# A six-sublayer encoder trunk on one core: inputs and output laid out on the host instead of turned on the chip, and the first loads split

## The chip, the core and the metric

One core of a Trainium2 chip. The metric is the device time of one launch in microseconds (us), median of several runs. TensorE (PE) multiplies, ScalarE (ACT) and VectorE (DVE) work element by element, GpSimd (POOL) does a little copying, SyncE (SP) issues most of the DMAs. A name with a q behind it (SPq, ACTq) is the engine's own sequencer, on which its DMAs are issued.

## What is computed

256 tokens of width 1024, with 16 learned meta tokens ahead of them (272 columns), go through two layers. Each layer is a SwiGLU block, a mixer (stick-breaking attention in the first, sliding-window attention with sinks in the second) and another SwiGLU block, each between two RMS norms. Everything is float32.

```python
def swiglu(x, w_gate, w_up, w_down):
    return (jax.nn.silu(x @ w_gate) * (x @ w_up)) @ w_down

h = jnp.concatenate([meta, x], axis=1)
for i in range(DEPTH):                       # DEPTH = 2
    g = norm_g[i]
    f = swiglu(rms_norm(h, g[0]), ffn_w_gate[i, 0], ffn_w_up[i, 0], ffn_w_down[i, 0])
    h = h + 0.5 * rms_norm(f, g[1])
    m = mixer(rms_norm(h, g[2]))             # stick-breaking, then sliding window
    h = h + rms_norm(m, g[3])
    f = swiglu(rms_norm(h, g[4]), ffn_w_gate[i, 1], ffn_w_up[i, 1], ffn_w_down[i, 1])
    h = h + 0.5 * rms_norm(f, g[5])
return h[:, N_META:]
```

## The kernel before

The engines run programs written out by hand, each its own, and meet at semaphores. The residual stream `xT` lies with the 1024 features on the partitions, as 8 tiles of 128 features x 272 tokens (index `d` or `k`), so that every product contracts over partitions.

The weights come as 158 **panels** of 1 MB (128 x 2048 floats): a panel is 256 output columns of an input matrix with all 8 feature tiles, or 256 rows of an output matrix. `load` (L309) on SP brings panel g into one of two buffers `raw`, as soon as `conv_lo` has read the panel two before it. A panel of an input matrix is made of 1 KB runs in memory (256 floats of a row), a panel of an output matrix of 4 KB runs. Float32 products are made of two halves each: ACT casts a panel to `w_hi` (`conv_hi`, L403, two halves of 1024 columns), DVE subtracts it from the panel to get `w_lo` (`conv_lo`, L583), and PE adds three products, `w_lo*y_hi`, `w_hi*y_hi` and `w_hi*y_lo` (L887 to L889, and in the first panels of a sublayer L931, L933 and L940). The activations are split in the same way: ACT scales `xT` with the norm's gain into `y_hi` (L422), DVE makes `y_lo` (`y_low`, L594).

**The start.** SP issues the tokens (1 MB, one token per row, into `sq`) and then panel 0; panel 1 waits until the small tables have landed (L340). ACT issues four small DMAs: the first 256 columns of the constants (an identity and a matrix of ones), the meta tokens, the norm gains as 96 rows, and the sinks as one row. PE turns the tokens: for each feature tile one small and two full transposes into a PSUM bank (L902, L904), between them one transpose for the gains (L897) and one product with ones that spreads the sinks (L898). ACT casts panel 0, copies gains and sinks out of PSUM (L449, L450) and then makes `y_hi`; DVE makes `w_lo` of panel 0, then copies each turned tile to `xT` (L625) and follows with `y_low` of the tile before. PE takes panel 0 tile by tile (k from 0 to 7, with both output tiles), then panel 1, panel 2, the sum for the norm (L988), panel 3 and so on. The other 792 KB of the constants, which are first needed in the attention, are issued by ACT behind the last `y_hi` (L425).

**The end.** After the last product DVE updates `xT` tile by tile (L851, L859, with 256 tokens). PE turns each tile back (L1196) into four PSUM banks, one for each half of the tokens and half of the features; ACT copies three of them out (L578), DVE the last (L879), and SP stores each quarter (256 KB) when it is copied (L365).

```python
            for n, (a, half) in enumerate(OUT_PARTS):
                if n < 3:
                    sp_eng.wait_ge(out_a, n + 1)
                else:
                    sp_eng.wait_ge(out_d, 1)
                sp_eng.dma_start(out_v[a, :, 512 * half:512 * half + 512],
```

Of the kernel before, what the change touches and what calls it, by code (L numbers as in the profile page):

```python
# [25 lines left out]
P = 128  # L26
# [54 lines left out]
FEW = 2 * P  # L81
# [38 lines left out]
OUT_PARTS = [(0, 0), (1, 0), (0, 1), (1, 1)]  # L120
# [3 lines left out]
def build(nc, x_in, meta_in, norm_g, w_gate, w_up, w_down, sb_w_in, sb_w_out,  # L124
          swa_w_in, swa_sinks, swa_w_out, const_in, out):
    ctx = ExitStack()
    with ctx:
# [25 lines left out]
        g_rows = sb("g_rows", [DEPTH * 6 * KT, P])  # L153
        s_row = sb("s_row", [1, NH])
# [44 lines left out]
        def x_rows(t):  # L199

            return t[:].rearrange("p a b -> p (a b)")[:, 0:2 * D].rearrange("p (a n) -> p a n", a=2)

        def meta_rows(t):
            return t[0:META].rearrange("p a b -> p (a b)")[:, 0:D]

        few_landed = sem("few_landed")
        const_in_sem = sem("const_landed")
        x_landed = sem("x_landed")
        small_landed = sem("small_landed")
        raw_landed = [sem(f"raw_landed{i}") for i in range(RAW_SLOTS)]  # L210
# [3 lines left out]
        small_T = sem("small_T")  # L214
        small_ready = sem("small_ready")
        x_turned = sem("x_turned")
# [60 lines left out]
        out_turned = sem("out_turned")  # L277
        out_a = sem("out_a")
        out_d = sem("out_d")
# [25 lines left out]
        @block.sync  # L305
        def _(sp_eng):
            sp_eng.dma_start(x_rows(sq), x_in.rearrange("(a p) d -> p a d", p=P)).then_inc(x_landed, 16)

            def load(g, more, src):  # L309

                if g >= RAW_SLOTS:
                    sp_eng.wait_ge(lo_ready, 2 * (g - RAW_SLOTS + 1) + 2 * more)
                sp_eng.dma_start(raw[:, g % RAW_SLOTS, :].rearrange("p (k n) -> p k n", n=src.shape[-1]), src)\
                      .then_inc(raw_landed[g % RAW_SLOTS], 16)

            def columns(wt, i):

                return wt.rearrange("(k p) n -> p k n", p=P)[:, :, bass.ds(256 * i, 256)]

            def rows(wt, i):  # L320

                return wt.rearrange("(r c p) n -> p r c n", c=2, p=P)[:, bass.ds(i, 1)].rearrange(
                    "p r c n -> p (r c) n")

            def pairs(lo, n, body):

                with sp_eng.Fori(0, n // 2) as it:
                    for c in range(2):
                        body(lo + c, 2 * it, 2 * it + c)
                if n % 2:  # L330
                    body(lo + n - 1, 0, n - 1)

            for t in SUBS:
                if t.kind == "ffn":
                    j = t.part // 2
                    if t.u == 0:
# [5 lines left out]
                        with sp_eng.Fori(1, 11) as it:  # L342
                            load(2, 2 * it - 2, columns(w_gate[0, 0], it))
                            load(3, 2 * it - 2, columns(w_up[0, 0], it))
                    else:
                        with sp_eng.Fori(0, 11) as it:
                            load(t.g0, 2 * it, columns(w_gate[t.layer, j], it))
                            load(t.g0 + 1, 2 * it, columns(w_up[t.layer, j], it))
                    pairs(t.g_out, 11, lambda g, more, i: load(g, more, rows(w_down[t.layer, j], i)))
                else:  # L350
                    w_in, w_out = (sb_w_in[0], sb_w_out[0]) if t.kind == "sb" else (swa_w_in[0], swa_w_out[0])
                    if t.kind == "sb":
                        pairs(t.g0, t.n_in, lambda g, more, i: load(g, more, columns(w_in, i)))
                    else:
                        for i in range(t.n_in):
                            load(t.g0 + i, 0, columns(w_in, SWA_PANELS[i]))
                    pairs(t.g_out, t.n_out, lambda g, more, i: load(g, more, rows(w_out, i)))

            out_v = out.rearrange("(a p) d -> a p d", p=P)
            for n, (a, half) in enumerate(OUT_PARTS):  # L360
                if n < 3:
                    sp_eng.wait_ge(out_a, n + 1)
                else:
                    sp_eng.wait_ge(out_d, 1)
                sp_eng.dma_start(out_v[a, :, 512 * half:512 * half + 512],  # L365
                                 x_rows(sq)[:, a, 512 * half:512 * half + 512]).then_inc(out_stored, 16)
            sp_eng.wait_ge(out_stored, 64)
# [34 lines left out]
        def _(a):  # L402
            def conv_hi(g, it=0):  # L403
# [8 lines left out]
                for c in range(2):  # L412
                    part = slice(c * HALF, (c + 1) * HALF)
                    nc.scalar.copy(w_hi[:, g % SLOTS, part], raw[:, g % RAW_SLOTS, part]).then_inc(hi_ready, 1)  # L414
# [843 lines left out]
```

## Time and profile before

| | |
|---|---|
| median of 3 runs | 1123.28 us (1122.22 to 1127.62) |
| span of the profiled execution, first to last instruction | 1119.9 us |
| PE busy | 1080.2 us (96%) |
| DVE busy | 653.1 us (58%) |
| ACT busy | 503.3 us (45%) |
| PE's mean granted clock, as a share of full speed | 0.990 |
| read from memory, written | 167.78 MB, 1.05 MB |

The profiled execution is known by its span; the runs' times cover a little more than a span. The parts of the profile are: busy time of each engine, the chain of waits that ended last, groups of instructions by line, waits by who waited for whom, the DMA queues with the time from issue to landing, a timeline of instructions, and a table by stretches of time. Matmuls are pipelined, so the durations of neighbouring ones overlap; the distance of their starts tells the pace.

### The profile page before, as it was taken

To read this page: it belongs to the slowest core of one execution; us is meant where nothing else is said; L and a number is where in the kernel's file an instruction comes from. 1 tells how busy PE (TensorE), PEld (TensorE's weight loads), DVE (VectorE), ACT (ScalarE), POOL (GpSimd) and SP (SyncE) were. 2 spreads that over 40 slices of the span, in tenths; PEclk is the share of its full clock that TensorE was granted. 3 is DMA by queue.
4 is the path that set the end of the run, shared out by engine and by line. 5 is a ranking of instruction groups with operands and counts; after the bars stand their busy time and mean duration, and the time that the engine had idled before them with its cause. 6 is when DMAs were issued, how large, how long until landed. Compare 5 with 4: busy or idle time off the path is not lost.

```text
span 1119.9 us, 20564 instructions
## 1 busy us (share of the span) xinstructions
PE 1080.2 (96%) x8367; PEld 1045.7 (93%) x8367; DVE 653.1 (58%) x875; ACT 503.3 (45%) x710; POOL 10.9 (1%) x17
## 2 busy tenths in 40 slices
PE   7999999999999999999999999999997999999997
PEld 6999999899877899999998999999896789999996
DVE  5575553576565477555437765544687667755433
ACT  4554343444344455444334544433553746544422
POOL 0000000000000000000000000000011000000000
PEclk9999999999999999999999999999998999999998
DMA  7576555436300427654452665545340054765531
GB/s 232 177 229 188 166 173 188 150 114 225 113 1 1 151 77 225 186 187 156 183 186 78 189 211 165 186 169 170 113 152 37 4 186 125 236 202 187 188 113 38
DMA packets 125720, 169.62 MB, mean 151 GB/s; under 512 B 2674, under 2 KB 111442, under 8 KB 125666
## 3 DMA queue, kind: packets, MB, share of 16 engines
q1 hardware_dynamic: 125232, 167.78, 46.1%
q10 hardware_dynamic: 434, 1.06, 0.3%
q8 instruction: 41, 0.67, 0.3%
q14 instruction: 13, 0.11, 0.0%
HBM read 167.78 MB, written 1.05 MB: 151 GB/s over the span
## 4 chain that ended last, share of the span: by engine, by line
PE 93%; DVE 4%; ACT 1%; DMA 1%; issue 0%; SPq 0%; DVEq 0%; ACTq 0%
PE ps L887 25%; PE ps L889 25%; PE ps L888 25%; PE ps L1030 3%; PE ps L931 3%; PE ps L933 2%; PE ps L940 2%; PE ps L1048 1%; PE ps L1011 1%; PE ps L1113 1%; DVE w_lo L591 1%; PE ps L1182 1%; PE ps L1099 1%; DMA raw<-in_ffn_w_gate_dram 1%; PE ps L1084 1%; DVE scaled L851 0%
## 5 line engine op out<-in xcount | busy, mean ns | idle before, releaser
L414 ACT CAST w_hi<-raw 128x1024 fp32r<-128x1024 f32 x316 | 315.6, 1047 | 443.7 <-PE ps L889 337.6
L591 DVE TENSOR_TENSOR w_lo<-raw,w_hi 128x1024 fp32r<-128x1024 f32 x316 | 375.1, 1229 | 236.2 <-ACT w_hi L414 235.6
L887 PE MATMUL ps<-y_hi,w_lo 128*128 128x272 f32 (+1 forms) x1600 | 461.4, 288 | 2.9 <-DVE y_lo L737 1.0
L889 PE MATMUL ps<-y_lo,w_hi 128*128 128x272 f32 (+1 forms) x1600 | 459.8, 287 | 0.0
L888 PE MATMUL ps<-y_hi,w_hi 128*128 128x272 f32 (+1 forms) x1600 | 458.1, 286 | 0.0
L887 PEld LDWEIGHTS ps<-y_hi,w_lo 128*128 128x128 f32 x1600 | 301.3, 188 | 4.2 <-issue 3.5
L888 PEld LDWEIGHTS ps<-y_hi,w_hi 128*128 128x128 f32 x1600 | 301.4, 188 | 0.3
L889 PEld LDWEIGHTS ps<-y_lo,w_hi 128*128 128x128 f32 x1600 | 301.4, 188 | 0.0
L888 PE MATMUL ps<-h_hi,w_hi 128*128 (+2 forms) x704 | 201.6, 286 | 0.0
L887 PE MATMUL ps<-h_hi,w_lo 128*128 (+2 forms) x704 | 201.6, 286 | 0.0
L889 PE MATMUL ps<-h_lo,w_hi 128*128 (+2 forms) x704 | 200.9, 285 | 0.0
L887 PEld LDWEIGHTS ps<-h_hi,w_lo 128*128 128x128 f32 x704 | 132.7, 188 | 0.0
L889 PEld LDWEIGHTS ps<-h_lo,w_hi 128*128 128x128 f32 x704 | 132.5, 188 | 0.0
L888 PEld LDWEIGHTS ps<-h_hi,w_hi 128*128 128x128 f32 x704 | 132.4, 188 | 0.0
L931 PE MATMUL ps<-y_hi,w_lo 128*128 128x272 f32 (+1 forms) x224 | 60.2, 298 | 11.7 <-DVE y_hi L867 11.7
L650 DVE TENSOR_TENSOR hid<-act,ps 128x544 f32<-128x544 f32 (+1 forms) x44 | 31.2, 710 | 66.1 <-PE ps L889 66.1
L645 DVE TENSOR_TENSOR act<-ps,rms_inv 128x544 f32<-128x544 f32 (+1 forms) x44 | 31.5, 716 | 53.3 <-PE ps L889 49.1
L933 PE MATMUL ps<-y_hi,w_hi 128*128 128x272 f32 (+1 forms) x224 | 59.3, 294 | 0.0
L931 PEld LDWEIGHTS ps<-y_hi,w_lo 128*128 128x128 f32 x224 | 44.0, 196 | 14.0 <-DVE y_hi L867 13.8
L933 PEld LDWEIGHTS ps<-y_hi,w_hi 128*128 128x128 f32 x224 | 44.0, 196 | 0.0
L422 ACT ACTIVATE y_hi<-xT,gains 128x272 fp32r<-128x272 f32 (+1 forms) x43 | 22.3, 521 | 33.7 <-DVE xT L859 30.3
L940 PE MATMUL ps<-y_lo,w_hi 128*128 128x272 f32 (+1 forms) x224 | 35.6, 292 | 0.0
(106 smaller groups left out, 712.9 us busy)
## 6 DMA issues: line engine op xcount, KB each, us to landing
raw<-in_ffn_w_gate_dram SPq DMA_DIRECT2D x44, 1024.0 KB, 5.4
raw<-in_ffn_w_up_dram SPq DMA_DIRECT2D x44, 1024.0 KB, 5.4
raw<-in_ffn_w_down_dram SPq DMA_DIRECT2D x44, 1024.0 KB, 4.9
raw<-in_sb_w_in_dram SPq DMA_DIRECT2D x12, 1024.0 KB, 5.2
raw<-in_swa_w_in_dram SPq DMA_DIRECT2D x6, 1024.0 KB, 5.1
raw<-in_sb_w_out_dram SPq DMA_DIRECT2D x4, 1024.0 KB, 4.9
raw<-in_swa_w_out_dram SPq DMA_DIRECT2D x4, 1024.0 KB, 5.0
sq<-in_x_dram SPq DMA_DIRECT2D x1, 1024.0 KB, 5.8
```

The costliest lines, as they stand in the source:

```text
L414: nc.scalar.copy(w_hi[:, g % SLOTS, part], raw[:, g % RAW_SLOTS, part]).then_inc(hi_ready, 1)
L422: nc.scalar.activation(y_hi[:, d, t0:L], xT[:, d, t0:L], ACT.Copy, scale=gains[:, SUBS[b].pre + d:SUBS[b].pre + d + 1]).then_inc(yh_ready, 1)
L591: nc.vector.tensor_tensor(w_lo[:, g % SLOTS, part], raw[:, g % RAW_SLOTS, part], w_hi[:, g % SLOTS, part].bitcast(F32), ALU.subtract).then ...
L645: nc.vector.tensor_tensor(act[:, j % 2, :, t0:L], ps[:, b0:b0 + 2, t0:L], spread(rms_inv, 2, t0), ALU.mult).then_inc(gate_ready, 1)
L650: nc.vector.tensor_tensor(hid[:, j % 2, :, t0:L], act[:, j % 2, :, t0:L], ps[:, b0:b0 + 2, t0:L], ALU.mult).then_inc(h_ready, 1)
L887: nc.tensor.matmul(dst, w_lo[:, slot, pc], yh, start=first, stop=False)
L888: nc.tensor.matmul(dst, w_hi[:, slot, pc], yh, start=False, stop=False)
L889: return nc.tensor.matmul(dst, w_hi[:, slot, pc], yl, start=False, stop=last)
L931: nc.tensor.matmul(dst, w_lo[:, g % SLOTS, pc], y_hi[:, k, t0:L], start=(k == 0), stop=False)
L933: nc.tensor.matmul(dst, w_hi[:, g % SLOTS, pc], y_hi[:, k, t0:L], start=False, stop=False)
L940: nc.tensor.matmul(ps[:, BANK_IN[i][c], t0:L], w_hi[:, g % SLOTS, pc], y_lo[:, k, t0:L], start=False, stop=False)
L1030: mm = nc.tensor.matmul(ps[:, 2 + h % 2, at - back:at + width], cst("tri" if m == n else "ones"), sp[:, h % 2, src - back:src + width], st ...
```

## The change

All inputs are laid out on the host, ahead of the launch:

- The tokens come with the meta tokens ahead and already turned, as 128 x 8 x 272, in two DMAs straight into `xT` (tiles 0 to 3, tiles 4 to 7). The 28 transposes and products of the start, the PSUM copies L625, L449 and L450 and their semaphores are gone; `y_hi` and `y_low` of the first sublayer wait for the DMAs instead.
- Gains and sinks come as 128-partition tables by DMA (48 KB and 8 KB). The sinks are waited for only in the second attention.
- All 158 panels are one array in the order of use, each 128 rows of 8 KB. SP's program is five DMAs and then one loop with two loads a turn.
- Panel 0 is loaded in two halves, each with a semaphore, and the tokens' halves stand between and behind them. Panel 1 no longer waits for the small tables.
- All 920 KB of the constants are one DMA on ACT's queue, second in line at the start. PE waits for it ahead of the first norm sum.
- The output is stored as it lies, 8 stores of 128 KB, each when its tile of `xT` is updated; the host turns it back. The 16 transposes L1196 and the four copies L578 and L879 are gone.

```diff
 @block.sync
-            sp_eng.dma_start(x_rows(sq), x_in.rearrange("(a p) d -> p a d", p=P)).then_inc(x_landed, 16)
...
-                        load(0, 0, columns(w_gate[0, 0], 0))
-                        sp_eng.wait_ge(small_landed, 32)
-                        load(1, 0, columns(w_up[0, 0], 0))
...
+            sp_eng.dma_start(raw[:, 0, 0:HALF], panel(0)[:, 0:HALF]).then_inc(first_landed, 16)
+            sp_eng.dma_start(xT[:, 0:4, :], x_in[:, 0:4, :]).then_inc(x_landed[0], 16)
+            sp_eng.dma_start(raw[:, 0, HALF:PW], panel(0)[:, HALF:PW]).then_inc(raw_landed[0], 16)
+            sp_eng.dma_start(xT[:, 4:KT, :], x_in[:, 4:KT, :]).then_inc(x_landed[1], 16)
+            sp_eng.dma_start(raw[:, 1, :], panel(1)).then_inc(raw_landed[1], 16)
+            def load(g, it):
+                sp_eng.wait_ge(lo_ready, 2 * (g - RAW_SLOTS + 1) + 4 * it)
+                src = panels_in[bass.ds(2 * it + g, 1)].rearrange("g p n -> (g p) n")
+                sp_eng.dma_start(raw[:, g % RAW_SLOTS, :], src).then_inc(raw_landed[g % RAW_SLOTS], 16)
+            with sp_eng.Fori(0, PANELS // 2 - 1) as it:
+                for c in range(2):
+                    load(2 + c, it)
+            for d in range(KT):
+                sp_eng.wait_ge(x_ready, KT * 5 + d + 1)
+                sp_eng.dma_start(out[:, d, :], xT[:, d, META:L]).then_inc(out_stored, 16)
+            sp_eng.wait_ge(out_stored, 16 * KT)
 @block.scalar
-            a.dma_start(const[:, 0:FEW], const_in[:, 0:FEW]).then_inc(few_landed, 16)
-            a.dma_start(meta_rows(fT), meta_in).then_inc(x_landed, 16)
-            a.dma_start(g_rows[:], norm_g.rearrange("l n (k p) -> (l n k) p", p=P)).then_inc(small_landed, 16)
-            a.dma_start(s_row[:], swa_sinks).then_inc(small_landed, 16)
+            a.dma_start(gains[:], gains_in).then_inc(small_landed, 16)
+            a.dma_start(const[:], const_in).then_inc(const_in_sem, 16)
+            a.dma_start(sinks[:], sinks_in).then_inc(sinks_landed, 16)
             nc.scalar.preload_act_table_set("natural_log_exp_and_others")
+            a.wait_ge(first_landed, 16)
             conv_hi(0)
-            a.wait_ge(small_T, 1)
-            nc.scalar.copy(gains[:], ps[:, 7, 288:288 + 96]).then_inc(small_ready, 1)
-            nc.scalar.copy(sinks[:], ps[:, 7, 384:384 + NH]).then_inc(small_ready, 1)
-            a.wait_ge(small_ready, 2)
+            a.wait_ge(small_landed, 16)
             split_y(0)
 @block.vector
             conv_lo(0)
+            v.wait_ge(small_landed, 16)
             for d in range(KT):
-                v.wait_ge(x_turned, d + 1)
-                nc.vector.tensor_copy(xT[:, d, :], ps[:, d, 0:L]).then_inc(x_ready, 1)
...
+                v.wait_ge(x_landed[d // 4], 16)
+                y_low(0, d)
```

What now stands in two engines' programs. On DVE at the start, before (w_lo is the low half of the panels, y_lo that of the activations):

```order
L591 TENSOR_TENSOR w_lo<-raw,w_hi 128x1024 x2
L625 COPY xT<-ps 128x272 x2
L597 SCALAR_TENSOR_TENSOR y_lo<-xT,gains,y_hi 128x272
L625 COPY xT<-ps 128x272
L597 SCALAR_TENSOR_TENSOR y_lo<-xT,gains,y_hi 128x272
```

and in the changed kernel:

```order
L533 TENSOR_TENSOR w_lo<-raw,w_hi 128x1024 x2
L539 SCALAR_TENSOR_TENSOR y_lo<-xT,gains,y_hi 128x272 x8
L533 TENSOR_TENSOR w_lo<-raw,w_hi 128x1024 x4
L550 TENSOR_TENSOR fT<-fT 128x1088
```

The eight copies out of PSUM that stood between the `y_lo` steps are gone. On ACT at the start, the changed kernel has:

```order
L391 DMA gains<-in_gains_dram 128x96
L392 DMA const<-in_const_dram 128x1840
L393 DMA sinks<-in_sinks_dram 128x16
L394 ACT_TABLE_LOAD
L362 CAST w_hi<-raw 128x1024 x2
L373 ACTIVATE y_hi<-xT,gains 128x272 x8
L362 CAST w_hi<-raw 128x1024 x4
```

The large load of the constants, which stood behind the eight `y_hi`, has moved ahead of all of ACT's work; both casts of panel 0 still stand ahead of the first `y_hi`.

## Rows read from the trace of the kernel before

**Rows 1.** The page: busy time, and the two groups that split the panels.

```profile
PE 1080.2 (96%) x8367; PEld 1045.7 (93%) x8367; DVE 653.1 (58%) x875; ACT 503.3 (45%) x710; POOL 10.9 (1%) x17
...
L414 ACT CAST w_hi<-raw 128x1024 fp32r<-128x1024 f32 x316 | 315.6, 1047 | 443.7 <-PE ps L889 337.6
L591 DVE TENSOR_TENSOR w_lo<-raw,w_hi 128x1024 fp32r<-128x1024 f32 x316 | 375.1, 1229 | 236.2 <-ACT w_hi L414 235.6
```

**Rows 2.** Waits of PE: who waited for whom, us in total, times, longest.

```profile
PE ps L931 <- DVE y_hi L867: 11.7, 5, 2.4
PE ps L902 <- DMA fT<-in_meta_tokens_dram: 7.4, 1, 7.4
...
PE ps L887 <- DVE w_lo L591: 0.3, 1, 0.3
```

**Rows 3.** Timeline of the start: start us, duration us, engine, instructions, idle before.

```profile
0.75 0.44 SPq L307 DMA_DIRECT2D sq<-in_x_dram  x1
...
7.38 0.26 PE L902 MATMUL ps<-const,fT 16*128 16x16 f32 x1 [7.38 <-DMA fT<-in_meta_tokens_dram]
...
9.94 1.99 ACT L414 CAST w_hi<-raw 128x1024 fp32r<-128x1024 f32 x2 [5.78 <-DMA raw<-in_ffn_w_gate_dram]
...
11.01 2.36 DVE L591 TENSOR_TENSOR w_lo<-raw,w_hi 128x1024 fp32r<-128x1024 f32 x2 [11.01 <-ACT w_hi L414]
...
13.82 0.93 ACT L422 ACTIVATE y_hi<-xT,gains 128x272 fp32r<-128x272 f32 x2 [1.68 <-DVE xT L625]
...
14.40 0.59 PE L931 MATMUL ps<-y_hi,w_lo 128*128 128x272 f32 x1
...
15.47 0.66 PE L940 MATMUL ps<-y_lo,w_hi 128*128 128x272 f32 x2
...
18.64 0.43 PE L931 MATMUL ps<-y_hi,w_lo 128*128 128x272 f32 x1
...
19.06 0.29 PE L931 MATMUL ps<-y_hi,w_lo 128*128 128x272 f32 x1
...
19.18 0.28 PE L933 MATMUL ps<-y_hi,w_hi 128*128 128x272 f32 x1
...
22.97 0.39 PE L887 MATMUL ps<-y_hi,w_lo 128*128 128x272 f32 x1 [0.26 <-DVE w_lo L591]
```

**Rows 4.** Stretches of the start: after the busy times, PE's clock, DMA share and GB/s.

```profile
0.00:3.50 3.50, 0.00 (x0) 0.00 (x0) 0.00 (x0) 0.62 (x1) 0.20 (x4) 1.00 0.41 107
3.50:5.50 2.00, 0.00 (x0) 0.00 (x0) 0.00 (x0) 0.66 (x1) 0.00 (x0) 1.00 1.01 410
5.50:9.50 4.00, 2.12 (x9) 1.46 (x10) 0.00 (x0) 0.00 (x0) 0.00 (x0) 1.00 1.06 309
```

**Rows 5.** DMA issues: count, KB of each, median us from issue to landing.

```profile
raw<-in_ffn_w_gate_dram SPq DMA_DIRECT2D x44, 1024.0 KB, 5.4
...
raw<-in_ffn_w_down_dram SPq DMA_DIRECT2D x44, 1024.0 KB, 4.9
...
sq<-in_x_dram SPq DMA_DIRECT2D x1, 1024.0 KB, 5.8
out_dram<-sq SPq DMA_DIRECT2D x4, 256.0 KB, 2.2
```

**Rows 6.** Stretches in which PE's clock was at its lower level.

```profile
596.00:599.00 3.00, 2.90 (x13) 2.90 (x14) 3.00 (x9) 1.04 (x2) 0.00 (x0) 0.50 0.00 0
852.00:862.00 10.00, 7.06 (x30) 5.02 (x27) 7.71 (x25) 4.56 (x17) 0.71 (x1) 0.50 0.01 2
```

**Rows 7.** Timeline of the end.

```profile
1113.86 3.79 SPq L365 DMA_DIRECT2D out_dram<-sq  x4
1113.91 0.48 DVE L859 SCALAR_TENSOR_TENSOR xT<-scaled,gains,xT 128x256 f32<-128x256 f32 x1
...
1114.76 0.87 DVE L859 SCALAR_TENSOR_TENSOR xT<-scaled,gains,xT 128x256 f32<-128x256 f32 x2
...
1116.45 0.69 DVE L879 COPY sq<-ps 128x512 f32<-128x512 f32 x1 [0.81 <-PE ps L1196]
```

More of the change, by code:

```diff
@@ L359, in _, with panel @@
[L359 to L367, printed above, removed]
+            def panel(g):
+                return panels_in[g:g + 1].rearrange("g p n -> (g p) n")
@@ L412, in conv_hi @@
                 for c in range(2):
+                    if g == 0 and c == 1:
+                        a.wait_ge(raw_landed[0], 16)
                     part = slice(c * HALF, (c + 1) * HALF)
@@ L1235, in constants, with columns, rows, panels @@
     return c
+def columns(wt):
+    k, n = wt.shape
+    return wt.reshape(k // P, P, n // 256, 256).transpose(2, 1, 0, 3).reshape(n // 256, P, PW)
+def rows(wt):
+    k, n = wt.shape
+    return wt.reshape(k // 256, 2, P, n).transpose(0, 2, 1, 3).reshape(k // 256, P, PW)
+def panels(inputs):
+    parts = []
+    for t in SUBS:
+        if t.kind == "ffn":
+            j = t.part // 2
+            gate, up = columns(inputs["ffn_w_gate"][t.layer, j]), columns(inputs["ffn_w_up"][t.layer, j])
+            parts.append(np.stack([gate, up], axis=1).reshape(2 * len(gate), P, PW))
+            parts.append(rows(inputs["ffn_w_down"][t.layer, j]))
+        elif t.kind == "sb":
+            parts += [columns(inputs["sb_w_in"][0]), rows(inputs["sb_w_out"][0])]
+        else:
+            parts += [columns(inputs["swa_w_in"][0])[SWA_PANELS], rows(inputs["swa_w_out"][0])]
+    return np.ascontiguousarray(np.concatenate(parts))
 def kernel(**inputs):
@@ L1244 @@
     nc = _bacc.Bacc("TRN2", target_bir_lowering=False, num_devices=1)
+    given = {name: _np.asarray(a) for name, a in inputs.items()}
+    tokens = _np.concatenate([given["meta_tokens"], given["x"][0]])
+    laid = {
+        "x": _np.ascontiguousarray(tokens.T.reshape(KT, P, L).transpose(1, 0, 2)),
+        "gains": _np.ascontiguousarray(given["norm_g"].reshape(DEPTH * 6 * KT, P).T),
+        "sinks": _np.ascontiguousarray(_np.broadcast_to(given["swa_sinks"], (P, NH))),
+        "panels": panels(given),
+        "const": constants(),
+    }
     arrays, args = {}, []
[L1246 to L1247 removed]
+    for name, a in laid.items():
         arrays[f"in_{name}_dram"] = a
         args.append(nc.dram_tensor(f"in_{name}_dram", a.shape, _mybir.dt.from_np(a.dtype), kind="ExternalInput").ap())
[L1250 to L1255 removed]
+    args.append(nc.dram_tensor("out_0_dram", (P, KT, SEQ), F32, kind="ExternalOutput").ap())
+    build(nc, *args)
     r = _run(nc, [arrays], core_ids=[0])
[L1257 removed]
+    return _np.ascontiguousarray(r.results[0]["out_0_dram"].transpose(2, 1, 0).reshape(1, SEQ, D))
```

122 lines of the change are left out of this document (14 added, 108 removed).

## The prediction

> **What bounds the kernel now.** I read the busy shares first: PE works for 1080.2 us of a span of 1119.9 [rows 1], so all that any change to the other engines can give lies in the 40 us in which PE stands, or in PE work taken away. The waits of PE say where these 40 us are: 7.4 us in front of the first transpose, 11.7 us at the five joins between sublayers, and almost none, once 0.3 us, for a weight panel [rows 2]. So the panels are off the path: DMA, cast and subtraction keep ahead of PE everywhere but once at the start. What the change touches on the path is the first 23 us and the last 4.
>
> The timeline of the start shows the order of events. The tokens are issued at 0.75 and land 5.8 us later, at 6.55; PE turns them from 7.38; panel 0 is there at 9.9, when ACT begins to cast it; DVE subtracts from 11.01 to 13.37, and only then copies the first turned tile; ACT makes the first `y_hi` at 13.82, and PE's first product of weights starts at 14.40, 0.58 us behind that [rows 3, 5]. So it is not the turning on PE that holds the start, it is the copy out of PSUM that stands behind 2.36 us of subtraction on DVE. From 14.40 PE is the bound: it takes 6 products a tile, at a distance of about 0.225 us, 1.35 us a tile, while DVE needs some 0.76 us and ACT 0.46 us (0.93 for two) a tile. Products run at half the later pace: one lasts 0.43 us up to 18.64, and 0.28 us from 19.1 on, where the next starts 0.12 us behind it [rows 3]; over a panel I count 0.125 us. That is the 1.2 GHz level of the clock and then the 2.4 GHz level. (The stretches of the start show a granted clock of 1.00 [rows 4], which these durations contradict; at 596 to 599 us the clock is written as 0.50 and 13 products take 2.90 us, the same pace [rows 6].)
>
> At the end the last tile of `xT` is done at 1115.63, the last copy out of PSUM at 1117.14, and SP's fourth issue closes at 1117.65 [rows 7]; the store lands some 2.2 us after its issue [rows 5].
>
> **The change, part by part.**
>
> *Start.* PE's first product now needs the first `y_hi`, which on ACT stands behind both casts of panel 0; the second cast needs the second half of panel 0. So the landing of that half is the term. Ahead of it or beside it are in flight: gains 0.049 MB, first half 0.524, constants 0.942 (issued by ACT before SP issues the second half), first half of the tokens 0.557, sinks 0.008, and itself 0.524: 2.60 MB. The trace moved 0.37 MB by 3.5 us (106 GB/s) and then 410 GB/s while the runs were 4 KB long [rows 4]; all the large new runs are at least that long. (2.60 - 0.37) / 0.41 = 5.4 us, so the bytes are in at 8.9. From bytes to landing the trace has, by the same count, 1.1 us for the tokens (1.18 MB with the constants, in at 5.5, landed at 6.55) and about 0.7 for panel 0; I take 0.9: **landed at 9.8 to 9.9**. The halves therefore land about where the whole panel did; what was won by splitting is given to the 0.94 MB of constants. Bounds: without the constants ahead, 1.66 MB, 7.5; with everything at the 309 GB/s of the 1 KB runs [rows 4], 11.6. I take 9.85, since the constants are issued ahead.
>
> Then one cast, 1.0 us, to 10.9 (the other ran while the second half was on its way), and 0.58 us to PE's first product: **11.5 instead of 14.40, 2.9 us earlier**. `y_lo` of tile 0 comes after the subtraction of the second half (1.2 us, to 12.15) and itself (0.5), at 12.65; PE reaches it 1.07 us after its first product [rows 3], at 12.57. So 0.1 us is lost: 2.8. From then on DVE and ACT, now without the copies, are faster than PE by a wider margin. The removed instructions themselves (28 on PE, the eight copies L625, and L449 and L450) count for nothing more: all of them lie ahead of 14.40 or beside PE.
>
> *Panel 1.* PE waited 0.3 us for its second half of `w_lo` [rows 2, 3], because ACT casts panel 1 behind all eight `y_hi`. ACT now ends these at 10.9 + 3.7 = 14.6, one cast and both subtractions (1.0 + 2.4) end near 18.1, and PE wants them 8.3 us behind its first product (22.97 - 0.26 - 14.40), at 19.8. **0.3 us** won. The wait for the norm sum and for its variance ahead of panel 3 stays: squares and sums depend on the same casts and all move earlier together. The new wait of PE for the constants ahead of that sum is covered: they land by about 10 us, PE is there three panels after its first product. The sinks' wait in the second attention is covered by 800 us.
>
> *Clock.* PE now stands idle until 11.5, instead of running small products from 7.38. The trace shows that these 7 us of transposes did not raise the clock: it was at 1.2 GHz until 18.9 [rows 3]. Without them it rises as many microseconds behind the first product (4.5), or somewhat later. Bound from above: if it needs as long from PE's first instruction as before (11.5 us), all 48 products of panel 0 run at 0.225 us instead of 20 of them (4.5 / 0.225), which costs 28 x 0.1 = 2.8 us; from below, if the clock were up at once, it gains the 2.0 us that the 20 slow ones cost. I take a loss of 0.3, near the row that has no change. The Trainium skill ("TensorE: Matmul & The Clock Gate", Part 1: The HAM clock gate) has it that the slow clock is the default state, that sustained activity releases it, and that the moment differs from run to run. That speaks against removing early PE work; by it and with the upper bound the sum would be 2.5 us smaller.
>
> *Splitting the loads.* Two more DMAs stand ahead of the tokens' end. SP spends 0.44 us on an issue [rows 3] while the bytes of the one before move, so this is covered. The DMAs overlap: the tokens and the first constants were issued at the same time and 410 GB/s moved with both in flight [rows 4]. The Trainium skill ("DMA: Bandwidth & Descriptors", Rules for kernel authors) advises one DMA of 1 MiB or more and against small ones. If each added one cost another 2.2 us in series, as a store's landing [rows 5], the second half would land 4.4 us later and nearly all the gain would be gone; the overlap in the rows says no.
>
> *All the other panels.* 8 KB runs instead of 1 KB or 4 KB. 4 KB runs land in 4.9 us against 5.4 [rows 5], so perhaps 4.7 now. Nobody on the path waits for them: **zero**.
>
> *End.* Each tile is stored when it is updated. The tiles come every 0.85 us (1113.91, 1114.76), an issue takes 0.4 to 0.5 us, so SP keeps up, and the last store is issued at 1115.65 instead of some 1117.2, **1.5 us** earlier. The last store is half as large: 128 KB less at 400 GB/s is 0.3 us. **1.8 us** in all. Bounds: 1.0 if seven stores in front hold it up by the time that their bytes took before, 2.2 if nothing does.
>
> **Sum:** 2.8 + 0.3 - 0.3 + 1.8 = 4.6 us. The span goes from 1119.9 to 1115.3. The median of the runs is 3.4 us above the span of the profiled execution, and I leave that distance as it is: **1118.7 us**, 0.4% below 1123.28. Differences of under 0.5% (5.6 us, so down to 1117.7) are about what a measurement of this kernel can't tell from no change.
>
> **The rivals.**
>
> *Larger gain at the start.* The constants don't get ahead of the second half: it lands at 7.5, 2.3 us earlier. Or the clock rises early. For it: the meta tokens, issued by ACT at 1.2 us, landed behind the tokens, so ACT's queue does not always win. Against: SP's own transfers would have to pass 0.94 MB that was issued before them. 1116.4 or less. Chance 0.15.
>
> *Other clock in the middle.* The clock fell twice: for 3 us behind the join at 596 (13 products, 1.3 us lost) and for 10 us in the second attention, where PE waited in between; 30 products there, some 3 us lost at most [rows 6]. All later work shifts by some 3 us, and the falls may come or stay away. One fewer of the long ones gives 1115.7; a fall at each of the other four joins costs 5.2 and gives 1123.9. The runs before spread over 5.4 us, which is as much. Chance 0.13 for lower, 0.07 for higher.
>
> *Slow clock at the start for longer*, as bounded above: gain 2.1, 1121.2. Chance 0.1.
>
> *Slower: the panel loads become the bound.* All 158 panels now lie end to end in one array. If loads of this layout took longer, this is the point: two panels share the two buffers, and PE needs 2 x 48 x 0.125 = 12.0 us for them. A buffer's own round is issue 0.4, landing 5.4, two casts of which one is ahead of the first subtraction (1.05), two subtractions (2.46): 9.3 us [rows 1, 5]. So it decides from a landing of 8.1 us on, and each further microsecond costs 79 rounds x 1 us. At 8.5 us that is 30 us, 1149. Against it: longer runs landed sooner, not later. Chance 0.03.
>
> *It does nothing*: the second half lands at 12 or later, or the stores queue up; 1121 to 1123. Chance 0.07.
>
> **How the numbers follow.** The forecast, 1117.7 to 1120.7, has 0.45. Faster by over 0.5% hold the larger gain, the lower clock case and the edge of the forecast's own error: 0.15 + 0.13 + 0.04 = 0.32. Slower by over 0.5% (above 1128.9) needs the panel rival or several falls of the clock: 0.04. The rest, 0.64, is within 0.5%. The range takes in the bounds of the landing (7.5 to 11.6) and one clock fall either way: 1115.2 to 1122.6.
>
> **What would show it.** In the changed profile: the cast of the second half starts at 9.9 and the first product at 11.5; no wait of PE for `w_lo` of panel 1; short products (0.28 us) from about 16 us on; the first norm sum 3 us earlier; the last `xT` some 2.8 us earlier than before, the end 2.5 us behind it instead of 4.3. Wrong would be: the second half landed before 8.5 or after 11, a span that changed in the middle by more than a microsecond, or a wait of PE or ACT's idle time for panels that grew.

## The result, and the profile after

The changed kernel takes 1118.06 us (median of 7 runs, 1115.84 to 1122.69) against 1123.28 us (7 runs, 1122.22 to 1129.57): the ratio is 0.9946, with a 95% interval of 0.9924 to 0.9969. The interval lies below 1, so it is faster, by about half a percent. The profiled execution took 1115.84 us with a span of 1114.1, so a launch is 1.7 us longer than its span.

The page of the changed kernel, its first lines and its two groups that split the panels, beside [rows 1]:

```profile
span 1114.1 us, 20552 instructions
PE 1068.1 (96%) x8324; PEld 1038.9 (93%) x8324; DVE 649.6 (58%) x866; ACT 501.0 (45%) x705; POOL 10.9 (1%) x17
L362 ACT CAST w_hi<-raw 128x1024 fp32r<-128x1024 f32 x316 | 316.1, 1048 | 441.4 <-PE ps L823 358.0
L533 DVE TENSOR_TENSOR w_lo<-raw,w_hi 128x1024 fp32r<-128x1024 f32 x316 | 375.3, 1229 | 221.8 <-ACT w_hi L362 221.4
```

PE lost 12.1 us of busy time and the span 5.8 (5.89 before rounding): most of the removed PE work lay beside other waits. The waits of PE, beside [rows 2]:

```profile
PE ps L846 <- DVE y_hi L805: 11.7, 5, 2.4
PE ps L846 <- ACT y_hi L373: 11.4, 1, 11.4
PE ps L1015 <- DVE s L724: 3.2, 2, 2.8
```

The joins are as before, the wait for panel 1 is gone, and PE now starts with one wait of 11.4 us. (The last line is a wait in the second attention, which will matter below.) The timeline of the start, beside [rows 3]:

```profile
4.73 1.04 ACT L362 CAST w_hi<-raw 128x1024 fp32r<-128x1024 f32 x1 [1.28 <-DMA raw<-in_panels_dram]
...
9.89 1.04 ACT L362 CAST w_hi<-raw 128x1024 fp32r<-128x1024 f32 x1 [4.12 <-DMA raw<-in_panels_dram]
10.84 3.40 ACT L373 ACTIVATE y_hi<-xT,gains 128x272 fp32r<-128x272 f32 x8
10.96 1.23 DVE L533 TENSOR_TENSOR w_lo<-raw,w_hi 128x1024 fp32r<-128x1024 f32 x1 [3.94 <-ACT w_hi L362]
11.41 0.59 PE L846 MATMUL ps<-y_hi,w_lo 128*128 128x272 f32 x1 [11.41 <-ACT y_hi L373]
...
12.66 0.82 PE L855 MATMUL ps<-y_lo,w_hi 128*128 128x272 f32 x2
...
15.94 0.29 PE L846 MATMUL ps<-y_hi,w_lo 128*128 128x272 f32 x1
...
32.46 0.44 DVE L556 TENSOR_SCALAR pre_ms<-ps 128x272 f32<-128x272 f32 x1 [6.23 <-PE ps L904]
```

The kernel before has its last line at

```profile
35.84 0.44 DVE L614 TENSOR_SCALAR pre_ms<-ps 128x272 f32<-128x272 f32 x1 [2.80 <-PE ps L988]
```

ACT stands 4.1 us between its two casts, until the second half of panel 0 has landed at 9.87. The first product of weights starts at 11.41 instead of 14.40. The first norm sum, which DVE reads as soon as PE has made it, is there 3.38 us earlier (32.46 instead of 35.84).

The DMA issues, beside [rows 5], and three stretches: the bytes of the start (last two numbers: DMA share and GB/s), beside [rows 4], and the fall of the clock behind the same join, beside [rows 6]:

```profile
raw<-in_panels_dram SPq DMA_DIRECT2D x157, 1024.0 KB, 4.8
out_dram<-xT SPq DMA_DIRECT2D x8, 128.0 KB, 1.9
const<-in_const_dram ACTq DMA_DIRECT2D x1, 920.0 KB, 7.7
```

```profile
3.50:5.50 2.00, 0.00 (x0) 0.00 (x0) 0.00 (x0) 0.77 (x1) 0.00 (x0) 1.00 1.03 387
5.50:9.50 4.00, 0.00 (x0) 0.00 (x0) 1.22 (x1) 0.27 (x1) 0.00 (x0) 1.00 1.01 407
592.80:595.80 3.00, 2.93 (x13) 2.93 (x14) 3.00 (x10) 1.04 (x2) 0.00 (x0) 0.50 0.00 0
```

The end, beside [rows 7]:

```profile
1109.94 0.48 DVE L797 SCALAR_TENSOR_TENSOR xT<-scaled,gains,xT 128x256 f32<-128x256 f32 x1
1110.45 1.66 SPq L311 DMA_DIRECT2D out_dram<-xT  x3
1110.46 0.42 DVE L789 TENSOR_TENSOR scaled<-fT,post_f 128x256 f32<-128x256 f32 x1
1110.80 0.87 DVE L797 SCALAR_TENSOR_TENSOR xT<-scaled,gains,xT 128x256 f32<-128x256 f32 x2
```

The last update of `xT` ends at 1111.67, 3.96 us earlier than before (1115.63), and the span ends 2.4 us behind it instead of 4.3. So the 5.9 us between these two profiles are 3.4 at the start, 1.9 at the end, and 0.6 that came in between. The 0.6 is a net figure. The lead over the kernel before, taken between the same DVE instructions, goes from 3.38 at the first norm sum down to 3.03 at the end of the fourth sublayer, up to 3.43 behind the second attention, and to 3.96 at the end of the last sublayer.

### The profile page after: what moved, and what is told of

Same layout as the page of the kernel before. It is cut to its first block, busy times and chain, and to the rows that moved or that the text cites. A ratio compares the mean times of both kernels' runs of the same rounds, so it can differ in the third digit from the quotient of the medians.

```text
span 1114.1 us, 20552 instructions
## 1 busy us (share of the span) xinstructions
PE 1068.1 (96%) x8324; PEld 1038.9 (93%) x8324; DVE 649.6 (58%) x866; ACT 501.0 (45%) x705; POOL 10.9 (1%) x17
## 4 chain that ended last, share of the span: by engine, by line
PE 94%; DVE 3%; ACT 1%; DMA 1%; issue 0%; SPq 0%; DVEq 0%
PE ps L821 25%; PE ps L822 25%; PE ps L823 25%; PE ps L846 3%; PE ps L946 3%; PE ps L848 3%; PE ps L855 3%; PE ps L964 1%; PE ps L927 1%; PE ps L1029 1%; PE ps L1098 1%; PE ps L1015 1%; DMA raw<-in_panels_dram 1%; PE ps L1000 1%; DVE w_lo L533 1%; DVE scaled L789 0%
```

## The experiments

All times are medians with lowest and highest run. The kernel before was run beside each; its runs lay between 1121.5 and 1129.6 us. The lowest runs tell more than the medians here, for reasons that come out below, but not as they stand: the lowest run of the kernel before itself was 1122.22 us beside the changed kernel, 1121.56 beside the next four, 1121.54 beside padded to join_warm and 1122.11 beside the last two (the last three of these groups ran on three different chips). The last column takes this off. The medians of the kernel before were 1123.3 to 1123.5, but 1126.36 beside the last two, so their ratios look a quarter of a percent better than they are. For effects under 2 us I go by places in the profiles, which have a limit of their own (the clock at the start, below).

| kernel | runs | median | lowest to highest | ratio to before, 95% | lowest run, under the lowest of the kernel before |
|---|---|---|---|---|---|
| changed kernel | 7 | 1118.06 | 1115.84 to 1122.69 | 0.9946 [0.9924, 0.9969] | 6.38 |
| packed_only | 10 | 1122.46 | 1121.17 to 1127.80 | 0.9993 [0.9969, 1.0017] | 0.39 |
| old_end | 10 | 1118.81 | 1117.04 to 1124.83 | 0.9947 [0.9921, 0.9972] | 4.52 |
| const_late | 4 | 1113.92 | 1113.52 to 1115.59 | 0.9903 [0.9865, 0.9940] | 8.04 |
| whole | 7 | 1115.65 | 1115.10 to 1119.24 | 0.9924 [0.9899, 0.9949] | 6.46 |
| padded | 7 | 1115.92 | 1115.10 to 1120.60 | 0.9933 [0.9909, 0.9957] | 6.44 |
| warm | 10 | 1115.32 | 1114.12 to 1122.48 | 0.9934 [0.9914, 0.9954] | 7.42 |
| early_y | 4 | 1113.19 | 1111.39 to 1117.12 | 0.9896 [0.9861, 0.9930] | 10.15 |
| join_warm | 7 | 1116.56 | 1116.20 to 1118.16 | 0.9932 [0.9908, 0.9957] | 5.34 |
| best | 6 | 1112.40 | 1111.89 to 1117.84 | 0.9892 [0.9867, 0.9918] | 10.22 |
| best_join | 5 | 1112.21 | 1110.16 to 1114.20 | 0.9878 [0.9854, 0.9902] | 11.95 |

### packed_only: the panels alone

The kernel before with one array of panels:

```diff
-            for t in SUBS:
-                if t.kind == "ffn":
...
+            with sp_eng.Fori(0, PANELS // 2 - 1) as it:
+                for c in range(2):
+                    load(2 + c, it)
```

> The kernel before, with nothing changed but the weights: all 158 panels in one array of 8 KB runs, loaded by one loop; tokens, gains, sinks, constants and output as before. Theory (no engine on the path waits for a panel): landing 4.7 to 4.8 us instead of 4.9 to 5.4, the rest unmoved; first product at 14.0 to 14.4 us (panel 0 may land up to 0.4 us sooner), last update of xT and end of span within 0.7 us of the kernel before, span about 1119.5. Rival (the packed panels gave a part of the 5.8 us, such as the 0.6 us that the changed kernel gained behind its first 40 us): span 1118.5 or less, with the lag to the kernel before growing between 40 and 1100 us.

Measured: lowest run 1121.17, median 1122.46, no difference that can be told from the kernel before. The panels land in 4.8 us:

```profile
raw<-panels_dram SPq DMA_DIRECT2D x158, 1024.0 KB, 4.8
```

Its first norm sum is 0.2 us later than before, and the last sublayer gains nothing here. So the panels' layout, which is most of the change in the code, gives nothing that can be told, as the theory has it. But the first product of weights missed the expectation: it starts at 15.34, not at 14.0 to 14.4.

```profile
8.18 0.26 PE L864 MATMUL ps<-const,fT 16*128 16x16 f32 x1 [8.18 <-DMA fT<-in_meta_tokens_dram]
...
14.02 0.93 ACT L384 ACTIVATE y_hi<-xT,gains 128x272 fp32r<-128x272 f32 x2 [1.69 <-DVE xT L587]
...
15.01 0.69 PE L866 MATMUL ps<-const,sq 128*128 128x128 f32 x2
...
15.34 0.58 PE L893 MATMUL ps<-y_hi,w_lo 128*128 128x272 f32 x1
```

The meta tokens landed 0.8 us later in this execution (8.04 instead of 7.25), so PE turned its last tile only at 15.0, when the first `y_hi` had been there since 14.55. That 0.94 us was nearly all made good by the clock, which rose 2.8 us behind the first product instead of 4.6, so that 12 products were slow and not 20. Whether the layout of panel 0 delays the meta tokens, one profile can't tell. The profiled execution of this kernel happened to be one of its slowest, with a span of 1126.0. The table by stretches shows what 6 us more are made of (four more falls of the clock behind joins or in the first attention, at some 1.5 us each); the clock is the number behind the busy times, 0.50 in each of these rows:

```profile
223.00:226.30 3.30, 3.30 (x16) 3.30 (x16) 3.30 (x9) 1.52 (x3) 0.00 (x0) 0.50 0.00 0
305.00:308.00 3.00, 3.00 (x12) 2.54 (x12) 1.57 (x3) 1.13 (x2) 0.00 (x0) 0.50 0.00 0
397.20:400.20 3.00, 3.00 (x15) 3.00 (x15) 3.00 (x9) 1.14 (x3) 0.00 (x0) 0.50 0.00 0
602.00:605.00 3.00, 3.00 (x15) 3.00 (x15) 3.00 (x9) 1.44 (x3) 0.00 (x0) 0.50 0.00 0
```

The clock was at 1.2 GHz behind the joins at 223, 397, 602 and 807 us (the last not shown) and in the first attention, where the profiled execution of the kernel before was so only behind the join at 596 (and in the second attention, like all of them).

### old_end: the end undone

```diff
-                sp_eng.dma_start(out[:, d, :], xT[:, d, META:L]).then_inc(out_stored, 16)
+                sp_eng.dma_start(out_v[a, :, 512 * half:512 * half + 512],
+                                 x_rows(sq)[:, a, 512 * half:512 * half + 512]).then_inc(out_stored, 16)
```

with the transposes and the four copies back in place.

> The changed kernel with the old end: PE turns xT back, ACT and DVE copy, four stores of 256 KB. Theory: the start is untouched (first product at 11.4), the end of the span lies 4.3 us behind the last update of xT instead of 2.4, so the span is 1.9 us above the changed kernel's 1114.1, 1116.0. Rival (the end gives less, since eight stores only move the wait): 1114.5 to 1115.

Measured: in its profile the last update of `xT` ends at 1113.50 and the span at 1117.8, 4.3 us later, as in the kernel before; the changed kernel has 2.4. The lowest run, 1117.04, is 1.2 us above the changed kernel's lowest, and 1.9 with each set against the kernel before beside it (4.52 against 6.38). The end gives 1.9 us: the theory holds. The span itself (1117.8, not 1116.0) has one more fall of the clock behind a join, and a first norm sum 0.55 us later, since the clock rose 6.0 us behind the first product and not 4.4.

### const_late: the constants behind the start again

```diff
-            a.dma_start(const[:], const_in).then_inc(const_in_sem, 16)
...
                 if b == 0:
+                    a.dma_start(const[:], const_in).then_inc(const_in_sem, 16)
                     conv_hi(1)
```

> The changed kernel with the 920 KB of constants issued behind the eight y_hi again, as before the change. Theory (the second half of panel 0 waited for 0.94 MB of constants): it lands at 7.5 instead of 9.87, the first product starts at 9.1 instead of 11.4, and the span is 2.3 us shorter, 1111.8, less up to 0.5 us if a later panel now waits for the constants. Rival (ACT's queue does not delay SP's transfers, the half lands when it lands): first product at 11.4 and no change of the span.

Measured: the second half of panel 0 has landed when ACT casts it at 7.87 instead of 9.89, and the first product starts 2.0 us earlier:

```profile
7.87 1.04 ACT L362 CAST w_hi<-raw 128x1024 fp32r<-128x1024 f32 x1 [2.22 <-DMA raw<-in_panels_dram]
...
9.39 0.59 PE L846 MATMUL ps<-y_hi,w_lo 128*128 128x272 f32 x1 [9.39 <-ACT y_hi L373]
```

The first norm sum is 1.42 us earlier (31.04), not 2.0: the clock rose 5.8 us behind the first product instead of 4.4. Lowest run 1113.52, 2.3 us under the changed kernel's, 1.7 by the last column of the table. (The profiled span, 1113.8 and not 1111.8, has one more fall behind a join and that later rise.) So the constants did delay the start, nearly by the bytes that they have; moving them ahead is the one edit of the change that these runs show to have cost microseconds.

### whole: the loads not split

```diff
-            sp_eng.dma_start(raw[:, 0, 0:HALF], panel(0)[:, 0:HALF]).then_inc(first_landed, 16)
-            sp_eng.dma_start(xT[:, 0:4, :], x_in[:, 0:4, :]).then_inc(x_landed[0], 16)
-            sp_eng.dma_start(raw[:, 0, HALF:PW], panel(0)[:, HALF:PW]).then_inc(raw_landed[0], 16)
-            sp_eng.dma_start(xT[:, 4:KT, :], x_in[:, 4:KT, :]).then_inc(x_landed[1], 16)
+            sp_eng.dma_start(raw[:, 0, :], panel(0)).then_inc(raw_landed[0], 16)
+            sp_eng.dma_start(xT[:], x_in).then_inc(x_landed[0], 16)
```

> The changed kernel with panel 0 as one load and the tokens as one load behind it. Theory: panel 0 lands at about 9 (1.05 MB and the constants), tokens (3.15 MB in all) at 10.6 to 11.2; both casts are over when the tokens land, so y_hi follows at once and the first product starts at 11.2 to 11.8, at most 0.4 us later than with halves: the split is worth little as long as both casts stand ahead of y_hi. Rival (the split is what brought the start forward): first product at 13 or later, span 1.5 us or more above 1114.1.

Measured:

```profile
5.93 1.99 ACT L360 CAST w_hi<-raw 128x1024 fp32r<-128x1024 f32 x2 [2.49 <-DMA raw<-in_panels_dram]
...
10.89 3.41 ACT L371 ACTIVATE y_hi<-xT,gains 128x272 fp32r<-128x272 f32 x8 [2.96 <-DMA xT<-in_x_dram]
11.46 0.59 PE L844 MATMUL ps<-y_hi,w_lo 128*128 128x272 f32 x1 [11.46 <-ACT y_hi L371]
```

Panel 0 came sooner than I had said (5.93, not 9: most of the constants moved behind it), the tokens at 10.9; the first product is 0.05 us later than with halves, the first norm sum 0.26 us later. The split is worth nothing that can be measured in this order of casts: the first `y_hi` waits for the second half behind the constants, or for the tokens behind them, until nearly the same time. Its lowest run is 0.7 us below the changed kernel's, but so was that of the kernel before beside it; by the last column the two are equal (6.46 and 6.38).

### early_y: what the split could give

```diff
+                        if d == 4:
+                            conv_hi(0, part_of=1)
                         a.wait_ge(x_landed[d // 4], 16)
...
-            conv_hi(0)
+            conv_hi(0, part_of=0)
```

with the same on DVE (the second half's `conv_lo` ahead of `y_low` 4), and the constants late.

> The constants late, and ACT and DVE take tiles 0 to 3 of y_hi and y_lo between the first and the second half of panel 0, so that PE can begin when the first halves of panel and tokens are there. Theory (the order of the two casts ahead of y_hi makes PE wait for the second half): the tokens' first half lands near 6.2, first product at 6.8 against 9.4 with the constants late alone; PE then stands up to 1 us for the second half's w_lo (landed 7.5 to 7.9, cast, subtraction: 10.2) and less than 1 us for panel 1; first norm sum 1.5 to 2.5 us earlier than with the constants late alone. Rival (the start is bound by the bytes of panels 0 and 1, so an earlier first product only waits later): first norm sum less than 0.5 us earlier.

Measured: the first product starts at 6.92, and PE has no wait over 0.15 us until the norm sum; that is at 27.66, 3.4 us earlier than with the constants late alone (31.04) and 4.8 us earlier than in the changed kernel:

```profile
6.25 1.76 ACT L375 ACTIVATE y_hi<-xT,gains 128x272 fp32r<-128x272 f32 x4 [0.74 <-DMA xT<-in_x_dram]
...
7.92 1.04 ACT L362 CAST w_hi<-raw 128x1024 fp32r<-128x1024 f32 x1
...
6.92 0.57 PE L850 MATMUL ps<-y_hi,w_lo 128*128 128x272 f32 x1 [6.92 <-ACT y_hi L375]
```

That is more than I expected. The slow products run while the second half is on its way, and the clock rose 3.3 us behind the first product here, against 5.8 in const_late, which is luck and alone worth about 1 us (14 slow products against 24). Lowest run 1111.39, 2.1 us under const_late, in four runs each.

### warm: dense work ahead of the first product

```diff
+                if t.u == 0:
+                    pe.wait_ge(idle_set, 1)
+                    for _ in range(30):
+                        nc.tensor.matmul(ps[:, 7, 0:128], idle[:, 0:P], idle[:, 0:128], start=True, stop=True)
```

> The changed kernel with 30 float32 products of 128 columns (ones by ones, into an unused bank) on PE ahead of the first product of weights, some 9 us of work from about 1.5 us on; GpSimd sets their operand. Theory (PE's clock rises only behind some microseconds of dense work, and the removed transposes were not dense enough): the clock is at 2.4 GHz when the first product starts at 11.4, the 20 slow products become fast, and the span is 2.0 us shorter than 1114.1 plus or minus falls of the clock at the joins: 1112.1; panel 1's low half may then be a little late. Rival (the clock rises only with the real products, or the extra work delays the first product): no gain, span 1114 or more.

Measured: the clock rises at 6.9, and the first norm sum is 1.55 us earlier (30.91 against 32.46); lowest run 1114.12, 1.7 us under the changed kernel's, 1.0 by the last column. PE now reaches `y_lo` of the first tile 0.5 us too soon, which is the rest of the 2.0. So dense products ahead of the first one do bring the clock up in time: 7 us of transposes of the kernel before had left it at 1.2 GHz, here it rose behind 5.6 us of products. The expected gain is confirmed. That the transposes had no part at all in when the clock rose later is not shown by it.

**best** puts this (11 such products) and early_y together. (A float32 product of this kind is two rows in the trace.)

> Early y_hi with the constants late, and 11 float32 products of ones ahead of the first product (from 1.3 us to about 6.3). Theory: first product at 6.9 as with early_y, and the clock rises at 6.9 to 8 instead of 10.2, so that some 10 to 14 slow products become fast: 1.0 to 1.4 us less than early_y, lowest run 1110.1 to 1110.5 against 1111.39; the spread of 5 to 7 us by falls of the clock at joins stays, median about 1112. Rival: the filling ends too early or holds the first product up, lowest run 1111.4 or more.

Measured: lowest run 1111.89, median 1112.40: no gain over early_y that can be told, which is what the rival said, though for another reason. The clock is up at 4.9, the products run fast from the second on, and then PE waits:

```profile
PE ps L828 <- DVE w_lo L538: 1.6, 1, 1.6
```

Its norm sum is at 28.35, later than early_y's 27.66, because panel 1 landed later here (its cast at 11.99 instead of 11.30). With the early order the start is bound by the bytes of panel 1, and a faster PE only waits for them.

### join_warm and best_join: the joins filled

```diff
                 out_panel(t.n_out - 1, 0, last=True)
+                if t.u < 5:
...
+                    for _ in range(9):
+                        nc.tensor.matmul(ps[:, 7, 0:128], idle[:, 0:P], idle[:, 0:128], start=True, stop=True)
```

> The changed kernel with nine float32 products of 128 columns (ones by ones, into a bank that is free) at each of the five joins between sublayers, in PE's idle 2.7 us. The runs of the changed kernel lie between 1115.8 and 1122.7 with mean clocks of 0.991 to 0.985. Theory (the spread is the clock, which falls at a join in some runs and then costs 1.4 us a fall): no fall at any join in the profile, runs within 2 us of each other, median at or below 1115. Rival (the spread comes from elsewhere, or the filling delays the joins): same spread, or all runs later by up to 1 us a join.

Measured: seven runs within 2.0 us (1116.20 to 1118.16), where the changed kernel's seven spread over 6.9. In the profile the clock falls at no join; the filling ends 0.35 us ahead of the first product of the next sublayer and delays nothing. But it was at 1.2 GHz for 17 us in the second attention, instead of 10:

```profile
845.10:862.00 16.90, 14.06 (x55) 10.57 (x56) 11.34 (x32) 8.31 (x31) 1.34 (x1) 0.50 0.00 0
```

which costs 2.1 us of the lead (4.56 us at 855, 2.46 at 875), so the lowest run is no lower, and the median (1116.56) missed my 1115. In this profile and in best_join's no join has a fall, where each of the other ten has at least one: the filling removes it at the joins, and the attentions keep theirs. The 2.0 us that are left are not all clock (spans of 1114.4 and 1116.3 have mean clocks of 0.989 and 0.990), and a narrow spread in a few runs proves little: const_late's four lie within 2.1 us without any filling. That the filling lengthened the fall in the second attention is not shown either.

> The same with nine float32 products of ones at each join. Theory: no fall at a join, so the runs lie within some 2 us of each other; the lowest is 1110 to 1112, as the join filling did not lower the lowest run before (a longer fall in the second attention took it back), and the median is below that of the version without it by 0.5 to 1 us. Rival: the phase at which the clock looks is moved so that more time in the attentions is slow, and the median is no better.

Measured: 1110.16 to 1114.20, median 1112.21 against 1112.40: the spread is 4 us instead of 6, the medians can't be told apart in five and six runs. Both are faster than the kernel before and than the changed kernel; best_join has the lowest ratio, 0.9878 [0.9854, 0.9902], against a kernel before that had a high median beside it. Its profiled execution had one fall in the first attention (at 295 us) and none at a join.

### padded: the 0.6 us in between

```diff
         scaled = sb("scaled", [P, 2, L])
+        sb("unused_g", [96, P])
+        sb("unused_s", [1, NH])
```

> The changed kernel with two unused tiles (512 and 64 bytes a partition) where the kernel before had g_rows and s_row, so that all tiles behind them lie at the old addresses. It is about 0.6 us: the products of the last sublayer's output panels start 117.4 ns apart in the changed kernel and 118.5 ns in the kernel before, some 560 of them. Theory (the place of the tiles in a partition sets it): 118.5 ns again, and the last update of xT 0.6 us later relative to the first norm sum. Rival (something else of the new start or the host layout): 117.4 ns stays.

Measured: by the distances of the starts, 118.5 ns in the last sublayer's output panels, as in the kernel before and in packed_only, against 117.4 in the changed kernel, old_end, const_late and whole. The rows count it: 40 us of the same stretch in the changed kernel, and in the padded one.

```profile
1060.00:1100.00 40.00, 40.00 (x343) 40.00 (x342) 10.34 (x9) 9.38 (x11) 0.00 (x0) 1.00 0.23 79
```

```profile
1060.00:1100.00 40.00, 40.00 (x340) 40.00 (x340) 11.80 (x10) 9.47 (x10) 0.00 (x0) 1.00 0.27 94
```

So the pace follows the addresses: with `g_rows` and `s_row` gone, all tiles behind them (the hidden activations `h_hi` and `h_lo`, which the output panels are multiplied with, among them) moved by 576 bytes in each partition, and the 528 products of these panels got 1.0 ns shorter. Why the place matters stays open.

The other half of the expectation failed: the last update of `xT` is not 0.6 us later relative to the first norm sum. These two places in padded are

```profile
33.28 0.44 DVE L558 TENSOR_SCALAR pre_ms<-ps 128x272 f32<-128x272 f32 x1 [7.02 <-PE ps L906]
...
1113.18 0.87 DVE L799 SCALAR_TENSOR_TENSOR xT<-scaled,gains,xT 128x256 f32<-128x256 f32 x2
```

which is 1080.8 us, 1.6 more than in the changed kernel (1079.2). But 1.5 of it is a fall behind the join at 219 us, which the changed kernel's profile doesn't have. What is left is under 0.1 us. The lead over the kernel before, sublayer by sublayer, tells why:

| lead gained, us | changed kernel | padded |
|---|---|---|
| SwiGLU sublayers 1, 3 and 4 | -0.15 each | 0.00, 0.00, -0.01 |
| first attention sublayer | +0.15 | +0.14 |
| second, to the norm sum behind it | +0.40 | +0.36 |
| last SwiGLU sublayer | +0.53 | +0.01 |

(The joins add -0.05 in the changed kernel and nothing but the fall in padded.) The new addresses give 0.53 us in the last sublayer and take 0.15 in each of the other three, where a product of an output panel takes 125.2 ns instead of 124.9. In sum they give under 0.1 us. The 0.6 us in between come mostly from the two attentions, and they come at the old addresses too. In the second, one wait of PE of 0.3 us is gone (before, at 883 us):

```profile
PE ps L1099 <- DVE s L786: 3.6, 3, 2.9
```

against 2 waits and 3.2 us in the changed kernel, and 2 and 3.3 in padded. What made it go, and the rest, is not shown.

## Why the prediction was right, step by step

- *What held the start before* the change is read too narrowly. The prediction says that it is not the turning on PE but the copy out of PSUM. The trace has both ending together:

```profile
13.82 0.93 ACT L422 ACTIVATE y_hi<-xT,gains 128x272 fp32r<-128x272 f32 x2 [1.68 <-DVE xT L625]
...
13.99 0.69 PE L904 MATMUL ps<-const,sq 128*128 128x128 f32 x2
```

  The first `y_hi` is there at 14.34, the second of PE's last two transposes starts at 14.26, and the first product follows at 14.40 without a wait; in packed_only it was the turning that came last. The change removes both, so the sum doesn't suffer. (The start had 27 rows of such PE work, not 28.)
- *The landing of the second half*: 9.8 to 9.9 by the bytes ahead of it, 9.87 measured. That the constants stand ahead was the right choice between 7.5 and 11.6, and const_late showed the lower bound to be nearly what one gets without them (landed at 7.84). The prediction took the 0.94 MB to be all ahead; the rate was 387 and 407 GB/s instead of 410.
- *The first product*: 11.5 predicted, 11.41 measured. *`y_lo` of tile 0*: 12.65 predicted, 12.66 measured; since the first product came 0.09 us sooner than predicted, PE lost 0.2 us there and not 0.1. At the end of panel 0 the lead is 2.86 us, where the prediction has 2.5 with its clock term. *Panel 1*: the wait is gone, as said, and it had cost 0.4 us by the distance of the starts (22.43 to 22.97), not 0.3. That is 3.3 of the 3.38 measured.
- *Clock at the start*: the loss of 0.3 us that I took was not there in the profiled execution; it rose 4.4 us behind the first product, 4.6 before. That is luck. The changed start was profiled four times with nothing different in it (changed kernel, old_end, padded, join_warm): the clock rose 4.4, 6.0, 6.5 and 4.3 us behind the first product, and the first norm sum came at 32.46, 33.01, 33.28 and 32.30. The lead at the start is therefore 2.6 to 3.5 us, 3.1 in the mean, with 2.8 predicted. Whether the removed transposes helped the clock stays open: with them it rose 4.6 us (kernel before) and 2.8 us (packed_only) behind the first product, without them and without filling 3.3 to 6.5 us in seven profiles. Two profiles on one side are too few. Dense work was shown to help (warm, 1.5 us). The rule of the Trainium skill ("TensorE: Matmul & The Clock Gate", Part 1: The HAM clock gate), that sustained activity raises the clock at a moment that differs from run to run, agrees with these rows.
- *Splitting*: I called it covered, and found what it wins given to the constants. The runs say both: whole is 0.05 us later at the first product, and the split pays only in early_y, where the order of ACT and DVE makes use of it.
- *All the other panels, zero*: packed_only has 0.9993 [0.9969, 1.0017]. But the middle of the span was not zero: 0.6 us came there, 0.5 of it in the two attentions and under 0.1 from the addresses of tiles, terms that the prediction did not have.
- *End*: 1.8 us predicted, 1.9 measured (2.4 us behind the last update, 2.5 predicted).
- *Sum*: 4.6 us predicted, 5.9 between the two profiled spans: 0.6 from the middle, 0.3 from the clock that rose as before, 0.3 from the start's own terms, 0.1 from the end. The medians moved by 5.2. That the median came out within 0.6 us of 1118.7 is in part luck: the seven runs lie 6.9 us apart, and the interval of the ratio allows a gain of 3.5 to 8.5 us. The terms were confirmed one by one, the number only that closely.
- *The distance of 3.4 us between median and span* was a wrong reading, though it did little harm. A launch is 1.7 to 1.9 us longer than its span in the runs of all kernels but best (up to 2.0); by that the profiled execution before took some 1121.7, at the low end of its kernel's runs, and the rest of the distance is most likely falls of the clock that it did not have. It should have been made against the lowest runs: from 1122.22, or 1121.5 among all runs of the kernel before, to 1115.84 is 6.4 or 5.7; the spans have 5.9.
- *The clock in the middle*, which had 0.20 as a rival, is not a rival but what the medians are made of. Each run of the changed kernel has its span and mean clock: 1114.1 at 0.991, 1116.3 at 0.990, 1117.7 at 0.988, 1119.0 at 0.986, 1120.9 at 0.985 (and two more at 0.991, within 0.3 us of the first). From 0.991 to 0.985, 0.6% of the span is 6.7 us, and the span grew by 6.8: as far as three digits tell, the whole spread is time at half the clock. Both profiled executions happened to have one fall behind a join and one in the second attention, which makes them comparable.
- *Chances*: the ratio of 0.9946 lies just beyond the 0.5%, the difference of the medians (5.22 us) just within. I had 0.64 on within and 0.32 on beyond; with the interval from 0.9924 to 0.9969 the runs don't decide between the two.

## What to carry to other kernels

Count the bytes that stand ahead of the first thing that everybody waits for, on every queue: here 0.94 MB of constants that nobody needed for 20 us cost 2 us, more than the split loads and the packed panels gave together. A split load pays only if the consumer's order is split too. Where runs differ by more than the effect, compare places in the profile (first product, first sum, last update), and lowest runs against the lowest of a kernel that ran beside them, not medians of a few. Even places behind the rise of the clock moved by 1.0 us between profiles of the same start. And a lead followed sublayer by sublayer shows gains and losses that cancel in one figure.

## What the runs showed that I had not expected

- The clock of PE falls at joins in which PE stands only 2.4 us, in some executions and not in others of the same kernel; one fall costs 13 to 16 products at 0.225 us, which by the leads is 1.25 to 1.5 us, and the profiles show it at four joins and in both attentions. Nine small products in each gap kept it up in all joins of two profiled executions.
- The place of tiles in a partition, moved by 576 bytes, changed the pace of the output panels' products: from 118.5 to 117.4 ns in the last sublayer, and the other way, from 124.9 to 125.2 ns, in the other three SwiGLU sublayers, where a product is 272 columns wide and not 256. padded undid both. Another 2 KB ahead of the same tiles (warm, join_warm, best) changed nothing.
- A transfer on ACT's queue holds up those behind it on SP's: issued 0.5 us ahead of the second half of panel 0, the constants landed at 8.86 us, the half at 9.87, and they delayed it by 2.0 us of their 2.3 us. In whole, the 1 MB of panel 0 was issued 0.45 us ahead of the constants and landed at 5.91, and the constants at 10.99.
